# Queries' root carried by the exponentials, an unscaled difference of maps, and two attentions of a layer as two rows of units

## The reference, cut to what matters

```python
def rms_norm(x, w):
    xf = x.astype(jnp.float32)
    y = xf * lax.rsqrt(jnp.mean(xf * xf, axis=-1, keepdims=True) + NORM_EPS)
    return (y * w.astype(jnp.float32)).astype(x.dtype)
...
sc = jnp.einsum('bqhmd,bkhmd->bmhqk', qi, k, preferred_element_type=jnp.float32) * scale
sc = jnp.where(qpos[:, None] >= kpos[None, :], sc, NEG_INF)
p = jax.nn.softmax(sc, axis=-1)
pd = p[:, 0] - lam * p[:, 1]
return jnp.einsum('bhqk,bkhe->bqhe', pd.astype(v.dtype), v)
```

## Time and profile before

| what | us |
|---|---|
| median of 3 runs (1345.61 to 1351.86) | 1349.02 |
| the profiled execution | 1350.45 |
| its span, first to last instruction | 1348.6 |
| PE busy in it | 1291.3 (96%) |
| PE weight loads busy | 1065.4 (79%) |
| DVE busy | 922.1 (68%) |
| ACT busy | 653.7 (48%) |
| POOL busy | 114.0 (8%) |

### The profile page before, as it was taken

How to read it: one execution, slowest core, us unless ns; L and a number is a source line. 1 busy time by engine, 2 the same in 40 slices (tenths; PEclk the granted TensorE clock), 3 DMA queues, 4 the chain that set the end, 5 groups by cost and what they waited for, 6 DMA issues and landing times.

```text
span 1348.6 us, 15871 instructions
## 1 busy us (share of the span) xinstructions
PE 1291.3 (96%) x6342; PEld 1065.4 (79%) x6342; DVE 922.1 (68%) x1237; ACT 653.7 (48%) x884; POOL 114.0 (8%) x146
## 2 busy tenths in 40 slices
PE   8999999998999999999999899999999968999998
PEld 6878888887877888887788777888878756888886
DVE  6968777766787677775778747766667874744444
ACT  6645444442563544444564536545446553654542
POOL 2001000001001000000334100000004400000000
PEclk9999999999999999999999989999999988999999
DMA  9626677864634678884353205867755411444450
GB/s 377 236 75 227 240 304 302 319 247 156 213 115 147 207 295 307 310 307 162 112 189 125 79 32 189 323 268 272 289 218 187 157 63 34 183 171 183 180 187 32
DMA packets 41113, 270.35 MB, mean 200 GB/s; under 512 B 4656, under 2 KB 4672, under 8 KB 12880
## 3 DMA queue, kind: packets, MB, share of 16 engines
q1 hardware_dynamic: 38288, 259.83, 52.2%
q0 software_dynamic: 2464, 8.98, 1.8%
q10 hardware_dynamic: 288, 0.52, 0.1%
HBM read 268.27 MB, written 1.05 MB: 200 GB/s over the span
## 4 chain that ended last, share of the span: by engine, by line
PE 79%; DVE 12%; ACT 5%; issue 2%; POOL 1%; DMA 0%; ACTq 0%; DVEq 0%; POOLq 0%
PE ps L1573 47%; PE ps L1563 24%; PE ps L1587 4%; DVE WB L1888 3%; PE ps L1675 2%; ACT E L1688 1%; PE ps L1650 1%; ACT WB L1688 1%; DVE st L2104 1%; POOL st L1490 1%; ACT H L1688 1%; DVE st L2174 1%; DVE SCR L2006 1%; ACT XTH L1688 1%; DVE H L2258 0%
## 5 line engine op out<-in xcount | busy, mean ns | idle before, releaser
L1888 DVE TENSOR_TENSOR WB<-RAW,WB 128x2048 fp32r<-128x2048 f32 (+3 forms) x211 | 452.8, 2151 | 235.9 <-ACT WB L1688 235.6
L1688 ACT ACTIVATE WB<-RAW 128x2048 fp32r<-128x2048 f32 (+3 forms) x211 | 379.9, 1802 | 218.5 <-PE ps L1573 214.8
L1563 PE MATMUL ps<-WB,XTH 128*128 128x512 f32 (+3 forms) x1176 | 314.0, 388 | 9.3 <-ACT XTH L1688 4.4
L1573 PE MATMUL ps<-WB,XTH 128*128 128x512 f32 (+3 forms) x1176 | 306.6, 382 | 9.7 <-DVE WB L1888 9.6
L1573 PE MATMUL ps<-WB,XTL 128*128 128x512 f32 (+3 forms) x1176 | 304.4, 380 | 0.9 <-DVE XTL L1961 0.5
L1573 PEld LDWEIGHTS ps<-WB,XTH 128*128 128x128 f32 x1176 | 218.1, 189 | 53.8 <-DVE WB L1888 15.2
L1563 PEld LDWEIGHTS ps<-WB,XTH 128*128 128x128 f32 x1176 | 213.6, 190 | 49.5 <-ACT XTH L1688 7.8
L1573 PEld LDWEIGHTS ps<-WB,XTL 128*128 128x128 f32 x1176 | 219.0, 189 | 40.3 <-DVE XTL L1995 0.8
L1563 PE MATMUL ps<-WB,HTH 128*128 128x512 f32 (+1 forms) x452 | 126.9, 396 | 0.6 <-ACT HTH L1688 0.5
L1573 PE MATMUL ps<-WB,HTH 128*128 128x512 f32 (+1 forms) x452 | 126.5, 395 | 0.0
L1573 PE MATMUL ps<-WB,HTL 128*128 128x512 f32 (+1 forms) x452 | 126.4, 394 | 0.0
(11 more groups left out here) (179 smaller groups left out, 961.3 us busy)
## 6 DMA issues: line engine op xcount, KB each, us to landing
RAW<-W SPq DMA_DIRECT2D x220, 1024.0 KB, 4.9
RAW<-W SPq DMA_DIRECT2D x22, 768.0 KB, 4.3
VEC<-vecd POOLq DMA_DIRECT2D x10, 512.0 KB, 6.5
RAW<-W SPq DMA_DIRECT2D x8, 512.0 KB, 3.7
RAW<-W SPq DMA_DIRECT2D x4, 576.0 KB, 3.7
RAW<-W SPq DMA_DIRECT2D x2, 648.0 KB, 3.9
T<-sgwd POOLq DMA_DIRECT2D x2, 512.0 KB, 8.5
X<-xd SPq DMA_DIRECT2D x1, 1024.0 KB, 18.3
```

What stands on the lines that cost most here:

```text
L1563: eng.matmul(banks[b][:, 0:cw], x2[j][0], hi[:, j, c0:c0 + cw], start=first and j == 0, stop=False)
L1573: op = eng.matmul(banks[b][:, 0:cw], x2[j][0 if low_w else 1], (lo if low_w else hi)[:, j, c0:c0 + cw], start=False, stop=last and end and ...
L1688: return eng.activation(dst, src, f, **k)
L1888: eng.tensor_tensor(WB[:, it["raw"], 0:w], RAW[:, it["raw"], 0:w], WB[:, it["high"], 0:w].bitcast(F32), ALU.subtract).then_inc(*up("wl", n))
```

## The change

- **Queries' root.** In mla, diff and moba the queries are no longer multiplied by their root. It is the `scale` operand of the exponentials instead (a column of `RQ`, 1/8 or 96^-0.5 included), and `nb` is made with it. mla's queries are multiplied by their gain only in the 32 rotated columns; the gain of the other 64 is multiplied once into that of the keys (`both_norms`, POOL). dil is left as it was.
- **Difference.** `differ` leaves the first maps unscaled and adds c2 times the second, c2 being -lambda times the ratio of the two sums. The norm behind it takes the scale out again, so its eps is multiplied by the square of the sum (`diff_out`, two small DVE instructions more; `root` on POOL is one instruction instead of two).
- **Two rows.** Each layer of the second block calls `attention` twice, mla (or diff) and then dil (or moba). `linear_k` takes its steps as a list in which the transposes (a, t) and the product (a, t, 0) are steps of their own. The same list form is used in the first block. `quiet` is gone; `soon` puts one waiting low half right behind the scores of a step.

```diff
+                    left[t] -= 1
...
+                if k in soon:
+                    lows(old[:1])
...
-            fill = chain(gating(), out_start())
-            attention(units, fill, first=1, pads=(0, 2, 2))
+            fill = chain(gating(), linear_k("w_o", mo, put_o(0), turn_o, ((4, 0), (4, 0, 0), (0, 0), (0, 0, 0), (4, 1, 0),
+                                                                          (0, 1), (0, 1, 0))))
+            attention(units, fill, (1, 1, 1, 1, 2, 1, 1, 0), first=1, pads=(0, 2, 2))
...
-                ahead = {6: [lambda: turn_groups(0)]}
-                between = {0: [lambda: turn_heads(1)], 6: [lambda: turn_groups(1)]}
-                steps = (4, 3, 2, 2, 2, 1, 1, 0, 2, 1, 1, 1, 1, 1, 1, 1)
-                pads, flush, quiet = (), (0, 1, 2, 3, 6, 7, 8, 9, 10, 11), (4,)
+                attention(units, fill, (4, 3, 2, 2, 2, 0, 0, 0), ahead={0: [lambda: turn_heads(1, 0)]},
+                          between={0: [lambda: turn_heads(1, 1)], 5: [lambda: turn_groups(0)], 6: [lambda: turn_groups(1)]},
+                          flush=(0, 1, 2), soon=(5,))
+                run(fill)
+                units, between = [], {}
+                steps, flush, soon = (1, 1, 1, 1, 0, 0, 1, 1, 0, 0), (), (0, 1, 2, 3, 4, 5)
...
-                steps = (1, 1, 1, 1, 1, 1, 2, 1, 1, 1, 1, 1)
-                pads, flush, quiet = (0, 0, 0, 2), (0, 1, 5, 6, 7), (3,)
+                attention(units, fill, (1, 1, 1, 1, 0, 0), ahead=ahead, between=rotated, flush=(0, 1))
+                run(fill)
+                units, between = [], {0: [lambda: normed.pop(0)()], 1: [lambda: normed.pop(0)()]}
+                steps, flush, soon = (0, 1, 2, 1, 1, 1, 0, 0), (), (1, 2, 3, 4)
...
+                fill = chain(gain_0(), proj((0, 0), (0, 0, 0), (0, 1), (4, 0), (4, 0, 0), (0, 1, 0), (4, 1), (4, 1, 0)))
+            else:
+                fill = proj((0, 0), (0, 0, 0), (0, 1), (0, 1, 0), (4, 0), (4, 0, 0), (4, 1), (4, 1, 0))
...
+                            scale = u["roots"][0][:, k // n2, k % n2:k % n2 + 1]
...
-                eng.reciprocal(r4, u["s4"]).then_inc(*own.up())
+                eng.reciprocal(r4, u["s4"][:, 2:4]).then_inc(*own.up())
...
-                    eng.tensor_scalar(e1, e1, c2[:, n_:n_ + 1], None, ALU.mult).then_inc(*own.up())
...
-                    op = eng.scalar_tensor_tensor(out=e0, in0=e0, scalar=r4[:, n_:n_ + 1],
-                                                  in1=E[:, i, (2 + n_) * nk:(3 + n_) * nk], op0=ALU.mult, op1=ALU.add)
+                    op = eng.scalar_tensor_tensor(out=e0, in0=E[:, i, (2 + n_) * nk:(3 + n_) * nk], scalar=c2[:, n_:n_ + 1],
+                                                  in1=e0, op0=ALU.mult, op1=ALU.add)
```

More of the change, by code:

```diff
@@ L325, in advance @@
             loads()
-            if not cur["quiet"]:
-                lows()
+            lows()
             while cur["item"] < cur["load"] and most:
@@ L591, in program, with attention @@
         p_free = [[], []]
-        def attention(units, filler=None, steps=1, pads=(), first=0, ahead={}, between={}, flush=None, quiet=()):
+        def attention(units, filler=None, steps=1, pads=(), first=0, ahead={}, between={}, flush=None, soon=()):
             n = len(units)
@@ L658, in attention @@
             for k in range(n + 2):
-                cur["quiet"] = k in quiet
                 for f in ahead.get(k, ()):
@@ L1192, in program @@
                 keys_, units = [], []
+                mla = units
                 for t in range(2):
@@ L1295, in out_start @@
-            def out_start():
-                for t in range(2):
-                    while "out" not in keys_[t]:
-                        yield
-                    if normed:
-                        normed.pop(0)()
-                    xo_w[t].extend(to_XT(MIX, 4, [keys_[t]["out"]], t))
-                    yield
-                    if t == 0 and i == 0:
-                        gain(0, 0)
-                        yield
-                yield from linear_k(nm_out, xo_w, gated_put(i, 0, 0, xg), ready, by_tile=i == 0)
@@ L1308, in program, with proj, gain_0 @@
-            fill = chain(fill, out_start())
+                    xo_w[t].extend(to_XT(MIX, n_out, [keys_[2 + t]["out"]], t, base=4))
+                else:
+                    xo_w[t].extend(to_XT(MIX, 4, [keys_[t]["out"]], t))
+            def proj(*steps):
+                return linear_k(nm_out, xo_w, gated_put(i, 0, 0, xg), turn_o, steps)
+            if i == 0:
+                def gain_0():
+                    gain(0, 0)
+                    yield
+                fill = chain(gain_0(), proj((0, 0), (0, 0, 0), (0, 1), (4, 0), (4, 0, 0), (0, 1, 0), (4, 1), (4, 1, 0)))
+            else:
+                fill = proj((0, 0), (0, 0, 0), (0, 1), (0, 1, 0), (4, 0), (4, 0, 0), (4, 1), (4, 1, 0))
@@ L1339, in program @@
                                               for kb in range(t + 1)]) for n_, h in enumerate(hh)]
-                        units.append(dict(banks=[segs[0:per], segs[per:]], joint=False, diff=False, same=True, after=tw2[t], scale=0.125,
+                        units.append(dict(banks=[segs[0:per], segs[per:]], joint=False, diff=False, same=True, after=tw2[t],
+                                          roots=(RQ[3, t][:, 2 * a:2 * a + 2 * per].rearrange("p (n m) -> p m n", m=2), ("odd", 3, t)),
                                           ok=ok, vafter=dw[5], sums=[SMd[t][:, h:h + 1] for h in hh],
                                           outs=outs, blocks=[c * 128 for c in range(2 * per * (t + 1))]))
-            attention(units, fill, steps, pads, 0, ahead, between, flush, quiet)
+            attention(units, fill, steps, (), 0, {}, between, flush, soon)
             t_pe = [keys_[3]["op"]]
```

159 lines of the change are left out of this document (98 added, 61 removed).

## The result

The changed kernel takes 1330.58 us in the median of four runs (1330.34 to 1331.26), against 1347.89 for four runs of the kernel before beside it: ratio 0.9869, 95% interval 0.9844 to 0.9894. That is 17.3 us less, 2.6 us above the forecast of 1328. Its profiled execution took 1330.73 us (span 1328.9, granted clock 0.992), 19.7 us less than that of before, where the sum said 20.8. PE is busy for 1283.7 us (97%) in place of 1291.3.

What follows compares the result with a forecast made beforehand. PE bounds the kernel, losing 29.2 us idle and 11.8 us to low clock in the attention stretches. Gains of 14.8 idle plus 6.0 clock, 20.8 us off 1350.45, give 1329.7 profiled, 1328 median; range 1319 to 1340.

Steps and rivals of the forecast that it cites:

- first block: Transposes one step ahead of their product cover PE's 0.78 us wait, in both layers: gain 1.6 us, bounds 0.8 and 2.
- DVE before the even row: Less multiplication of mla's queries on DVE brings low halves earlier at 694 to 718: gain 2.9 us, bounds 1.5 and 3.8.
- even rows, idle and clock: Even layer as two rows, mla then dil: idle 7.0 to 2.8 us, gain 4.2; its 6.0 us of clock back in full.
- odd first row: Odd layer's diff row: query multiplications and difference scalings go, differences come earlier: gain 2.7 us, bounds 1.5 and 4.2.
- odd seam, idle and clock: Odd layer between diff and moba rows: idle 14.2 to 10.8 us, gain 3.4, bounds -3 and 8; no clock back.
- nothing else opens: Even layer's later steps: with 1.5 + 0.7 + 0.7 us or more PE work per unit, no further waits appear.
- no wait over 0.8 us is left: Even layer: by the walk no longer wait remains, so its 6.0 us of clock loss was given back in full.
- the slower one: Rival: the seam keeps the clock at half through the whole second row, about +32 us, 1381; chance 0.03.
- Falls in both: Rival: the clock falls in both layers as before, gain 14.8 us, 1334; chance 0.20.
- the first rival: Rival: the clock stays up in both layers, gain 26.6 us, 1322; chance 0.22.
- The dear drains: Rival: row ends and beginnings wait for their chains in full, 6 to 8 us more idle, 1341; chance 0.10.
- doesn't do what it says: Rival: DVE's relief is off the path and gaps reappear behind the row; gain about 3 us, 1346; chance 0.05.

Runs made afterwards that it cites:

- late read-ahead: Kernel after with linear_k's read-ahead of weight items (whose high halves go to ACT) put behind the next transposes instead of in front: 1323.48 us, ratio 0.9813.
- kernel with unread products: Kernel after plus matrix products that nobody reads in the odd layer's waits (8, 6, 4 and 3): 1326.74 us, ratio 0.9838.
- arithmetic alone: Kernel before with only the change's arithmetic (queries' root in the exponentials, unscaled difference), in the old order of parts: 1343.92 us against 1347.52, ratio 0.9962.
- rows alone: Kernel after with the old arithmetic put back, leaving two rows and the new lists of steps: 1331.96 us, ratio 0.9880.

## Why the prediction was right, and where it was not

By the places of the same PE instructions before and after (the even row counts from the first product behind its first scores, 719.23 before and 715.06 after, so that the cover of those scores stands in the item that forecast it):

| step | forecast | measured |
|---|---|---|
| first block | 1.6 | 0.9 |
| DVE before the even row | 2.9 | 3.3 |
| even rows, idle and clock | 4.2 + 6.0 | 5.8 |
| odd first row | 2.7 | 2.9 |
| odd seam, idle and clock | 3.4 + 0 | 6.9 |
| sum | 20.8 | 19.8 |

The sum is better than its parts, and that is luck: the even rows gave 4.4 us less than forecast and the odd seam 3.5 more.

- *First block*: the cover was there. The step overlooked ACT's read-ahead, 0.4 us at each of two places; the late read-ahead showed it.
- *DVE before the even row*: right in place and size. The wait of 1.97 is 1.00, the two of 0.29 and 0.59 are gone, the gained transposes cover 0.9 of the 0.92 us before the first scores, and idle is 1.05 us where I had left 0.9. The cut multiplication takes 0.42 us (estimate 0.4).
- *Even rows*: the waits of the earlier trace rows went as told, and the drains between the rows cost little (0.43 and 0.17). The step that failed is "nothing else opens" and with it "no wait over 0.8 us is left": 2.15 and 1.26 us opened, idle became 5.5 and not 2.8, and the clock gave back 4.5 of its 6.0. I had walked the order of PE and DVE through the new list and not that of ACT's high halves. Of the changed `linear_k` I had costed its steps and not the `advance` at its head: a step that is moved issues all that stands in it. By my own signs this part of the prediction was wrong: it named a low clock in the dil row, and the clock was 0.91 over 760 to 780; and it said that no wait over 1 us would stand there.
- *Odd first row*: idle fell by 1.9 us (forecast 2.7; the pieces that I had named, 1.19 + 0.8 + 0.45 + 0.5, make 2.9), while the markers moved by 2.9: PE also has 1.0 us less work in the stretch (33.72 for 34.76), so the two lists don't begin and end on quite the same instructions. The waits at 1066, 1074 and 1081 are 0.42, 0.57 and 0.74 us.
- *Odd seam*: the mechanism was right (both waits of over 5 us gone, two shorter ones in their place, each with the releaser named), the size was off: idle 8.0 us and not 10.8. The two seam waits measured 2.44 and 1.95 (forecast 3.0 and 2.6), the last two 1.02 and 0.69 (1.2 and 0.7). Around the first product it was 1.60 + 0.15 for 0.5 + 0.7 + 0.7, for another reason: copies under a high half, as in the even layer. What was counted too high is, as I read it, the 1.0 us for the operand column, which is inside these waits and not on top of them (no run of the odd layer isolates it), and 0.4 for the last difference, which comes earlier, in the first row.
- *The clock*: forecast 6.0 back in the even layer and nothing in the odd; measured 4.5 and 0.9. It fell behind 2.15 us, 2.44 us and 1.02 + 0.69 us. One reading that I had built on was wrong: in the kernel before, the clock did not fall behind the wait of 2.11 us. It was 1.00 over 760 to 770 and 0.70 over 770 to 775, behind the 1.83. And the 5.8 us of the odd layer is too high as a price, since matmuls at the low clock that lie under a wait for another engine cost nothing (27.0 us for the seam at 0.83 as at 1.00, with the late read-ahead).
- *The median*: I took the profiled execution to lie 1.4 us above the median, as before's did. After's lies at its own (1330.73 and 1330.58). Of the 2.6 us by which the median missed, 1.3 is this and 1.1 the sum.

Of the rivals, the slower one is out: products of 512 columns ran at full clock again within the row. "Falls in both" came half true, and with the late read-ahead the clock stayed up in the even layer at least, at 1323.5 us, near the 1322 of the first rival. The dear drains didn't come in the even layer (0.43 and 0.17 us); "doesn't do what it says" is out by the 17.3 us.

## What to carry to other kernels

Where a list fixes the order of all engines, a step that is pulled apart moves everything it issues on every engine: walk each engine's stream, the helper that reads weights ahead included, and put long work with slack (a 1.9 us high half) behind the short copy that the next product waits for. That edit, a few lines, was worth 7 us here, twice the whole arithmetic. When a part is put later because it stands in front of something, move it on one engine and for one tile at a time: it lands in front of something else.

## What the runs showed of the hardware that I had not expected

The same wait does not always lower the clock. In the first block all versions have a wait of 2.07 to 2.11 us for a low half, with the same work around it. In the profile of the kernel after the clock fell behind it; in that of the kernel with unread products, which stand far later in the run, it didn't:

```profile
334.35 1.21 PE L1602 MATMUL ps<-WB,XTH 128*128 128x512 f32 x4 [2.10 <-DVE WB L1924]
335.40 1.67 PE L1616 MATMUL ps<-cst,X 128*128 128x128 f32 x8
```

```profile
334.87 1.20 PE L1619 MATMUL ps<-WB,XTH 128*128 128x512 f32 x4 [2.09 <-DVE WB L1941]
```

The granted clock over 330 to 340 was 0.83 in eight of the fourteen profiles (the first here and the kernel before among them) and 1.00 in six (the second here, the arithmetic alone and the rows alone among them). From this wait to the one for MIX at 345 it is 10.9 us in the one and 9.7 in the other. The even layer has another such place: the wait of 1.64 us before six transposes lowered the clock in the kernel before (0.56 over 785 to 790), and with the arithmetic alone, where the wait ahead of it is 1.27 us and not 1.83, a wait of 1.64 us left it at 1.00. So the length of one wait doesn't foretell the clock, and the forecast's "no wait over 0.8 us" is no limit that these runs show. It seems to bear on how runs spread as well: ten runs of the arithmetic alone lie between 1338.28 and 1346.31 us, with a mean granted clock of 0.992 in the fastest and 0.987 in the slowest, and its profiled run was the fastest of them, so its profile shows a gain of 12.2 us where the medians give 3.6. The kernel after spread by 0.9 us only. What decides at such a place is open; no run here isolates it. (The Trainium skill, TensorE: Matmul & The Clock Gate, Part 1, says of a kernel's start that the number of matmuls at the slow clock varies from run to run. No run here shows a start twice; these profiles, of different kernels, differ in the same way behind like waits in the middle.) A profile of one run should be set beside the median before a few us of clock are read from it.
